# Even layer: projections and attention in one stage, with the next pair's projections in halves between the attention units

## What is computed

```python
def forgetting_attention(q, k, v, log_f):      # 8 heads of 64, S = 512
    c = jnp.cumsum(log_f, axis=1).transpose(0, 2, 1)
    s = einsum(q, k) * Dh ** -0.5 + c[t] - c[s]       # masked to s <= t
    return einsum(softmax(s), v)

def multiscale_pool(u, pool_w, pool_scale):    # 4 groups of 128, windows 2, 4, 8, 16
    # trailing mean over the window (count min(t + 1, w)) minus the token,
    # then a 128 x 128 map per group and a scale per channel
    ...

def even_mixer(h, w_in, b_f, pool_w, pool_scale, w_out):
    q, k, v, f_logit, u = jnp.split(h @ w_in, [512, 1024, 1536, 1544], axis=-1)
    log_f = jax.nn.log_sigmoid(f_logit + b_f)
    attn = forgetting_attention(q, k, v, log_f)
    pool = multiscale_pool(u, pool_w, pool_scale)
    return jnp.concatenate([attn, pool], axis=-1) @ w_out
```

## Time and profile before

| | |
|---|---|
| median of 3 runs | 4335.34 us (4324.84 to 4347.59) |
| the profiled execution, its own time | 4330.66 us |
| its span in the trace | 4328.9 us |
| TensorE busy | 3842.3 us, 89% |
| VectorE busy | 2182.5 us, 50% |
| ScalarE busy | 892.6 us, 21% |
| mean granted TensorE clock | 0.951 |

### The profile page before, as it was taken

One profiled execution on the slowest core, in us unless ns is written; L12 is line 12 of the kernel. 1 busy time (PEld: TensorE's weight loads), 2 busy tenths in 40 slices (PEclk: granted clock), 3 DMA queues, 4 the chain that ended last, 5 costly groups with the idle time before them and its releaser, 6 DMA issues. The chain is left out here.

```text
span 4328.9 us, 68104 instructions
## 1 busy us (share of the span) xinstructions
PE 3842.3 (89%) x28492; PEld 2512.4 (58%) x28492; DVE 2182.5 (50%) x4276; ACT 892.6 (21%) x2134; POOL 427.7 (10%) x554
## 2 busy tenths in 40 slices
PE   6988988995999969899899598887889998989998
PEld 3577567772444435565687243333358877458877
DVE  2777577554222226576845433335264455564455
ACT  2244234411000011341630100001231001441000
POOL 0033013100111110430600000000000000000000
PEclk8999999997999989999999799998889999999999
DMA  6510420027999961211211899991211222121221
GB/s 218 185 36 12 175 89 17 21 99 277 388 388 384 391 213 43 84 54 71 87 69 49 327 397 400 400 404 61 90 44 59 87 88 93 39 102 59 88 88 54
DMA packets 244255, 674.39 MB, mean 156 GB/s; under 512 B 16601, under 2 KB 30566, under 8 KB 243950
## 3 DMA queue, kind: packets, MB, share of 16 engines
q1 hardware_dynamic: 233966, 653.26, 40.3%
q0 software_dynamic: 9984, 16.78, 1.8%
HBM read 652.85 MB, written 17.15 MB: 155 GB/s over the span
## 5 line engine op out<-in xcount | busy, mean ns | idle before, releaser
L3485 PE MATMUL bank<-weight_ring_extra_b,xs_b 128*32 128x512 f32 x3024 | 336.2, 594 | 16.9 <-DMA weight_ring_extra_b<-in_moe_w_up 16.8
L2675 PE MATMUL bank<-heads_out_b,swiglu_sums_b 128*128 128x256 f32 x1056 | 235.2, 379 | 3.9 <-DVE swiglu_sums_b L2722 3.9
L3485 PE MATMUL bank<-weight_ring,xs_b 128*32 128x512 f32 x1936 | 220.1, 604 | 16.6 <-DMA weight_ring<-in_moe_w_up 10.5
L3577 ACT ACTIVATE moe_silu_b<-bank 128x256 f32<-128x256 f32 x80 | 25.5, 383 | 966.7 <-PE bank L3485 966.7
L3485 PEld LDWEIGHTS bank<-weight_ring_extra_b,xs_b 128*32 128x32 f32 x3024 | 94.4, 110 | 223.0 <-issue 206.2
L2675 PEld LDWEIGHTS bank<-heads_out_b,swiglu_sums_b 128*128 128x128 f32 x1056 | 200.5, 190 | 31.8 <-issue 4.6
L3588 DVE TENSOR_SCALAR xs_b<-bank,factor_b,mod_b 128x64 f32<-128x64 f32 (+1 forms) x384 | 95.5, 324 | 228.1 <-PE bank L3469 228.1
L3542 PE MATMUL bank<-weight_ring_extra_b,moe_hidT_b 128*32 128x256 f32 x3104 | 176.7, 385 | 9.7 <-DMA weight_ring_extra_b<-in_moe_w_down 8.2
L3629 DVE TENSOR_TENSOR heads_out_b<-heads_out_b,bank 128x256 f32<-128x256 f32 x256 | 90.2, 415 | 174.1 <-PE bank L3522 174.0
L1661 POOL TENSOR_TENSOR d_level_b<-d_low_b,d_mask_b 128x256 f32<-128x256 f32 x144 | 116.4, 836 | 550.0 <-DVE d_far_b L1920 549.8
L2675 PE MATMUL bank<-hT_b,weight_ring 128*128 128x256 f32 x704 | 162.9, 385 | 3.2 <-PEq L192 3.2
(11 more groups left out here) (601 smaller groups left out, 7788.1 us busy)
## 6 DMA issues: line engine op xcount, KB each, us to landing
weight_ring_extra_b<-in_moe_w_down SPq DMA_DIRECT2D x38, 2048.0 KB
weight_ring_extra_b<-in_moe_w_gate SPq DMA_DIRECT2D x75, 1024.0 KB
weight_ring_extra_b<-in_moe_w_up SPq DMA_DIRECT2D x75, 1024.0 KB
weight_ring<-in_ada_w SPq DMA_DIRECT2D x24, 2048.0 KB
weight_ring<-in_moe_w_gate SPq DMA_DIRECT2D x48, 1024.0 KB
weight_ring<-in_moe_w_up SPq DMA_DIRECT2D x48, 1024.0 KB
weight_ring<-in_moe_w_down SPq DMA_DIRECT2D x21, 2048.0 KB
weight_ring<-in_ssd_w_in SPq DMA_DIRECT2D x12, 2048.0 KB
```

Source lines behind the costliest of these rows:

```text
L2675: last = pe.matmul(out, lhs[:, k, :], rhs[:, k, :], start=(k == 0), stop=(k == HK - 1))
L3485: last = pe.matmul(in_bank(g)[lanes[c], :], xs[:, e % 2, kt, g * GROUP:(g + 1) * GROUP], w[:, k, :, c * COLS:(c + 1) * COLS], start=(kt == 0),
L3577: last = act.activation(sl[:, g, :], in_bank(g)[:, 0:COLS], ACT.Silu)
```

## The change

One stage, `even_mix`, takes the place of two. The weights come in another order (f, v, k, q, u; the pool's weights no longer go through the ring). The stage begins with the gate's narrow product, the four v jobs and the first k and q job; the gate's running sum and the fetch of its rows stand between them. Then the 32 units follow as before, and the ten other jobs (three k, three q, four u) are cut into two halves of 8 matrix instructions, one half behind each unit where the table `EvenJobs` says so. Two banks (6 and 7) serve the jobs, and the values use one bank (5) in place of two. The window means, the pooled products ("mix") and their scaling stand between units too. The inverse counts are computed for 16 columns in place of 512. ScalarE moves the transposed rows in pieces of 128 columns (up to four a unit) in place of one instruction. One load fewer goes through the ring.

```diff
+class EvenJobs:
...
+    START = [("ev_v", t) for t in range(TX)] + [("ev_k", 0), ("ev_q", 0)]
...
+            for n, load in enumerate(("ev_k", "ev_q", "ev_u")):
+                self.add(p * parts + 2 * n, load, p if load == "ev_u" else p + 1)
+            self.pooled_at[(p + 1) * parts - 1] = p
+            if p:
+                self.add_mix(p * parts + 6, p - 1, (p + 1) * parts)
...
+        PT = core.sb(own, "probs_turned", 2, STRIDE * (TX - 1) + parts, P)
...
+            sp.dma_start(pool_weight[:], core.dram["ev_pool_w_2"][0].rearrange("g d e -> d g e")).then_inc(pool_loaded, 16)
+            core.ring.feed(sp, "ev_f")
+            kept = core.row_dram[0:FH * TX, :].rearrange("(h t) k -> h (t k)", t=TX)
...
+            def half_job(n, half):
+                load, c = table.jobs[n]
+                bank = core.bank[6 + n % 2]
+                if half != 1:
+                    wait_job_bank(n)
+                if load == "mix":
+                    pe.wait_ge(pool_loaded, 16)
+                    pe.wait_ge(summed, c + 1)
+                    pe.matmul(bank[:], pool_weight[:, c, :], pooled[:, c % 2, :], start=True,
+                              stop=True).then_inc(mixed, 1)
+                    return
+                core.ring.wait(pe, load)
+                w = core.ring.view(load)
                 cols = slice(c * P, (c + 1) * P)
-                for k in range(KT):
-                    lhs, rhs = (hT[:, k, cols], w[:, k, :]) if name == "ev_v" else (w[:, k, cols], hT[:, k, :])
-                    last = pe.matmul(core.bank[n % EVEN_BANKS][:], lhs, rhs, start=(k == 0), stop=(k == KT - 1))
-                last.then_inc(projected, 1)
-            core.ring.wait(pe, "ev_pool")
-            w = core.ring.view("ev_pool")
-            for g in range(groups):
-                pe.wait_ge(moved, 2 * EVEN_BANKS + g + 1)
-                pe.wait_ge(summed, g + 1)
-                pe.matmul(core.bank[g][:], w[:, g, :], pooled[:, g, :], start=True, stop=True).then_inc(mixed, 1)
+                for k in range(half * HALF_K, (half + 1) * HALF_K):
+                    lhs, rhs = (hT[:, k, cols], w[:, k, :]) if load == "ev_v" else (w[:, k, cols], hT[:, k, :])
+                    last = pe.matmul(bank[:], lhs, rhs, start=(k == 0), stop=(k == KT - 1))
+                if half:
+                    last.then_inc(projected, 1)
+
+            def job(n):
+                half_job(n, 0)
+                half_job(n, 1)
...
+                if s == 0:
+                    pe.wait_ge(moved, max(table.number("ev_k", p), table.number("ev_q", p)))
...
+            core.ring.wait(pe, "ev_f")
+            narrow.ready(pe, laid)
+            narrow.multiply(pe, core.ring.view("ev_f"), hT, multiplied)
+            job(0)
+            narrow.turn(pe, facc, copied).then_inc(gate_turned, 1)
+            job(1)
+            pe.wait_ge(gate_on_vector, 4)
...
+            for n in range(2, len(table.START)):
+                job(n)
+            pe.wait_ge(decays_copied, 1)
+            for u in range(len(units)):
+                score(u)
+                if u >= 2:
+                    turn(u - 2)
+                if u >= parts and u % parts == 4:
+                    values(u // parts - 1)
+                if u in table.at:
+                    half_job(*table.at[u])
...
+                for j in range(width(u) // P):
+                    last = act.activation(PT[:, p % 2, STRIDE * j + s, :], core.bank[3 + u % 2][:, j * P:(j + 1) * P], ACT.Copy)
+                last.then_inc(placed, 1)
...
+            act.wait_ge(weighed, 1)
+            for u in range(len(units)):
+                b, w = u % DEPTH, width(u)
+                if table.at.get(u - 1, (0, 0))[1] == 1:
+                    move_job(table.at[u - 1][0])
...
+            def pool_rows(g):
+                window, b = WINDOWS[g], g % 2
+                dve.wait_ge(moved, table.number("ev_u", g))
+                if g >= 2:
+                    dve.wait_ge(mixed, g - 1)
+                source, size, n = U[:, b, :], 1, 0
+                while size < window:
+                    rows = Ws[:, n % 2, :]
+                    linked(dve.tensor_copy(rows[:, 0:size], source[:, 0:size]))
+                    linked(dve.tensor_tensor(rows[:, size:], source[:, size:], source[:, 0:lead + NX - size], ALU.add))
+                    source, size, n = rows, 2 * size, n + 1
+                linked(dve.scalar_tensor_tensor(out=pooled[:, b, :], in0=source[:, lead:], scalar=1.0 / window,
+                                                in1=U[:, b, lead:], op0=ALU.mult, op1=ALU.subtract))
+                linked(dve.tensor_tensor(pooled[:, b, 0:lead], source[:, lead:2 * lead], inv[:, g, :], ALU.mult))
+                dve.tensor_tensor(pooled[:, b, 0:lead], pooled[:, b, 0:lead], U[:, b, lead:2 * lead], ALU.subtract) \
+                    .then_inc(summed, 1)
...
+                if u in table.scaled_at:
+                    scale_mixed(table.scaled_at[u])
...
+                if u in table.pooled_at:
+                    pool_rows(table.pooled_at[u])
...
+            scale_mixed(table.scaled_at[None])
...
+    ring.plan("ev_f", by_k(w, 3 * fw, 3 * fw + FH))
+    ring.plan("ev_v", by_k(w, 2 * fw, 3 * fw))
+    ring.plan("ev_k", by_k(w, fw, 2 * fw))
+    ring.plan("ev_q", by_k(w, 0, fw))
     ring.plan("ev_u", by_k(w, 3 * fw + FH, w.shape[1]))
-    ring.plan("ev_f", by_k(w, 3 * fw, 3 * fw + FH))
-    ring.plan("ev_q", by_k(w, 0, fw))
-    ring.plan("ev_k", by_k(w, fw, 2 * fw))
-    ring.plan("ev_v", by_k(w, 2 * fw, 3 * fw))
-    ring.plan("ev_pool", dram["ev_pool_w_2"][0].rearrange("g d e -> d g e"))
...
-            nlf = core.sb(inner, "neg_log_f", TX, FH)
-            even_project(core, hT, QT, KTt, U, V, catT[:, 4:8, :], nlf, "ev_pool", late)
-            forgetting_attention(core, QT, KTt, V, nlf, catT[:, 0:4, :], "ev_pool")
+            even_mix(core, hT, QT, KTt, U, V, catT[:, 4:8, :], catT[:, 0:4, :], "ev_u", late)
```

More of the change, by code:

```diff
@@ L2849, in _ @@
+            place(len(units) - 2)
+            place(len(units) - 1)
+            store(pairs - 1)
         @block.vector
```

337 lines of the change are left out of this document (161 added, 176 removed).

## The result

The changed kernel takes 4305.48 us (median of 7 runs, 4304.02 to 4312.22); the kernel before, on the same chip, 4329.20 us (7 runs, 4324.84 to 4354.64). The ratio is 0.9939, with a 95% interval from 0.9926 to 0.9953. The profiled execution took 4309.26 us (4330.66 before).

A forecast was written before the change was run, and what follows sets the result against it. TensorE was taken as the bound, waiting for VectorE in the attention. The new stretch summed to 186.0 us, 189.0 with two unknown costs, against 207.8: 18.8 less, so 4335.3 - 18.8 gives 4316 us, range 4304 to 4330 (8 in 10).

The forecast's parts named there:

- within 0.5%: Whole kernel: a measured time within 21.7 us of no change, given 58 in 100, against 36 for faster.
- two unknown costs: New stretch: entering halves, 0 to 3.7 us, and clock falls, 0 to 7.3; 3.0 us taken for both.
- head: Start of the stretch up to the first scores: narrow product 3.7, six jobs 41.2, gate, sum and copy; 49.7 us.
- last pair with values: Last units of the stretch: VectorE sets the pace from unit 26, 7.6 us of waiting, and 2.3 ahead of the values.
- entries: Starting a half after 64-row scores or transpositions: 0 to 3.7 us for 23 entries, 1 taken.
- clock term: TensorE's clock at pair boundaries and the end: one fall or a slow end, 2.0 us taken, bounds 0 and 7.3.
- boundary waits: Between pairs, parts 7 and 0 have no half to cover VectorE: 0.9 + 1.4 us first, about 1.65 at two others.
- upper bound: Clock cost if every pair boundary falls and the end runs at half rate: 7.3 us, time 4321.8.
- more is hidden: Rival, 24 in 100: new stretch at full clock, entries free, half the boundary waits gone; 183.2 us, time 4311.
- Little is hidden: Rival, 16 in 100: TensorE's in-order queue makes each half add to VectorE's chain; half hidden 201.7 us, time 4329.
- the clock stays down: Rival, 7 in 100: short waits keep the new stretch at clock 0.80, 41 us more work; time 4357.
- about 9 us are the wait for the decay rows: Account of the gain at the first attention unit: about 9 us from that wait, 2 from the barrier, rest waits and clock.

The follow-up runs named there:

- the repeat: The changed kernel itself measured and profiled once more, nothing changed: stretch 184.24 us, ratio 0.9949 to the kernel before.
- The run with half-size fillers: Changed kernel plus 11 throwaway products of 256 columns in the last pair's waits: 134.94 us from first scores to output stage against 135.11, ratio 0.9944.
- first kernel with early rows: Kernel before, both stages kept, running sum ahead of the last v job, write of the decay rows still queued behind waiting loads: stretch 213.4 us, ratio 1.0021.
- second kernel with early rows: Kernel before with the running sum early and the decay rows' write and reads ahead of the waiting loads: stretch 196.97 us, ratio 0.9976.

## Why the prediction was right or wrong

I had forecast 18.8 us less and "within 0.5%" as likelier than faster. It is 0.5 to 0.6% faster. The time of 4305.5 lies in the range, at its low end. It lies 10.5 us below the 4316; 6.1 of them are no error of the sum, since the three runs of before gave a median of 4335.3 and seven gave 4329.2.

**The sum, part by part** (us, from the first product of the stretch; the forecast is the terms of the sum laid on the parts, with none of the two unknown costs, and the measured parts hold whatever these were):

| part | forecast | measured |
|---|---|---|
| head | 49.7 | 49.12 |
| first pair | 29.2 | 29.66 |
| second pair | 34.1 | 34.33 |
| third pair | 35.1 | 35.11 |
| last pair with values | 36.4 | 34.36 |
| to the output stage | 1.5 | 1.65 |
| sum | 186.0 | 184.23 |
| entries, added to it | 1.0 | about 1, within the parts |
| clock, added to it | 2.0 | 0 to 0.2 |

**The step that failed** is the clock term of "Two costs that no row shows", laid beside the last pair's waits, which were too long themselves. The clock did fall, for more than I had taken: 3.3 us of slow products. But it fell in the last pair, in which TensorE waits for VectorE anyway. The sum already held 13.1 us of waits there (1.4 at the boundary, 1.8 for window means, 7.6 from unit 26 on and 2.3 ahead of the values), and I added 2.0 to them. The slow half stands exactly where the sum had its 1.8 us for window means after unit 23; in the repeat it was fast, the wait of 1.47 us stood there instead, and both stretches are 184.2 us long. The second fall stands in both profiles. The run with half-size fillers, at full clock throughout the last pair, is 0.2 us shorter, and no run shows more than that. Such a cost must be laid over the waits and not beside them. It was also asked in one direction only: that the clock would be up at the end, and that the output stage would then start 1.7 us faster than before, was in no term.

**The last pair** was 2.0 us too long in the sum, which is the second part of the miss. From unit 26 to the values the sum had 9.9 us of waiting (7.6 and 2.3). The trace has waits of 5.6 (0.86, 0.45, 2.04, 0.22, 0.83, 0.32, 0.88) and 1.6 us of slow products among them, 7.2 together. Of these only 1.2 are the last two waits, where I had 2.3. The products of the pair took some 0.7 us more than in the sum, which hides a part of this.

**Entries.** The 1.0 us was right, though not where it was looked for. A half behind a transposition takes 3.53 us from start to start where I had 3.43, and the transposition ahead of it gives the 0.1 back. Behind bare scores or behind values it takes 3.63, which happens four times, and the first mix behind values takes 1.05 where the others take 0.95.

**The head** was 0.6 too long. The narrow product took 2.91 us and not 3.7. I had misread the start of the stage before the change: not its first 8 records ran at half rate but 3 or 4 of them (the first 4 took 3.5 us, all 8 took 5.2).

**What held:** no wait for the decay rows, the head, boundary waits of 0.9 and 1.4 (0.89 and 1.32), the three lengths of pairs to 0.5 us, full clock up to unit 23 (I had said unit 25; the first slow half stands behind unit 24), and the loads. By the Trainium skill (TensorE: Matmul & The Clock Gate, "A second HAM failure mode: psum-queue depth-cycling") each boundary would have fallen and the upper bound stood. The traces agree with it where products stand alone between waits (bare pairs at 0.78 and 0.86, about 2 us a pair). Where a half follows each wait they agree only in part: of the three boundaries, with waits of 1.3 and 1.5 us, one fell in the first profile of the changed kernel and none in the second.

**Of the rivals**, the one in which more is hidden comes close in its number, 183.2 us against the 184.2 measured, and it was right that the clock would cost nothing. But the number is in part luck: the boundary waits that it took away are all there and the entries were not free, and what made up for them is the last pair, shorter than in any sum. "Little is hidden" and "the clock stays down" fell with the first two windows. Where the forecast's reasons were too simple is in its account of the gain: "about 9 us are the wait for the decay rows". The early rows are worth 10.9 us alone, but the halves would have covered that wait too, and cover, clock and rows don't add. That is why the sum of the new stretch could be nearly right while this list of reasons was not.

**Open:** what decides whether the clock falls after such a wait. In the first profile it fell after the 1.50 us at 3128.12 and not after the same wait at 3093.01 in the pair before; in the second it fell after neither. Since the kernel is the same, the cause lies outside of what these experiments varied.

## What to carry to other kernels

Work of a bound engine laid between the units of another engine's chain paid three times here: it filled the waits, TensorE's clock stayed up (worth 2 us in each bare pair of 18), and the chain got slack that swallowed a late transfer. Such gains cover one another and do not add. Price a cost over the waits that stand at its place, not beside them: a slow half of 1.7 us cost nothing inside a pair that waited, and slow last values, with nothing beside them, cost all of their 1.6 us. When a small result is moved earlier, look at the queue that carries it: the write of 16 KB left 10 us late behind loads that waited for something else, and the kernel became slower.

## What was not expected of the hardware

The write of the decay rows (16 KB, one DMA) and its completion, from its issue to the issue of the reads, took 1.47 us with no load issued for 18 us before it (changed kernel, 2999.39 to 3000.86), 5.29 us when a weight load of 2048 KB had been issued 4.7 us before (kernel before, 3096.05 to 3101.34), and 9.65 us when one had been issued 0.4 us before (first kernel with early rows, 3090.40 to 3100.05). The 16 DMA engines were busy 0.06, 0.89 and 0.95 of these times. The two rows of the changed kernel:

```profile
2999.39 0.30 SPq L2863 DMA_DIRECT2D decay_rows<-neg_c_b  x1
3000.86 4.99 SPq L2867 DMA_DIRECT2D neg_c_rows_b<-decay_rows  x8
```

So the small transfer took longer the closer it was issued behind a large one, while the DMA engines were busy; that it shares its way with it is the reading that fits. In the second kernel with early rows, with no load issued for 24 us, it took 1.48 us again. And a product that only fills a wait has a price of its own: 0.48 us for 256 columns (up to 0.54 from start to start), 0.97 for 512, since each such product stands in the trace as two records, and I had taken one record (0.43 us for 512 columns) for a product.
